# Two-layer SSD, attention and expert kernel: gather table, place of the gate exponent, and one set of transposes

## The reference

```python
def peer_ffn(h, w_q, keys, u_tab, v_tab):            # 8 heads, top 16, 128 x 128 experts
    q = (ht @ w_q).reshape(t, PEER_HEADS, 2, PEER_HALF)
    sc = jnp.einsum('thid,hikd->thik', q, keys)
    top_s, top_i = lax.top_k(sc, PEER_TOPK)
    cand = top_s[:, :, 0, :, None] + top_s[:, :, 1, None, :]
    best_s, best_pos = lax.top_k(cand.reshape(...), PEER_TOPK)
    experts = i1 * N_KEYS + i2
    gates = jax.nn.softmax(best_s, axis=-1)
    act = jnp.einsum('thkd,td->thk', u_tab[eb], hb)
    coef = gb * jax.nn.gelu(act, approximate=False)
    return jnp.einsum('thk,thkd->td', coef, v_tab[eb])
```

## Time and profile before

| | |
|---|---|
| median of three runs | 3040.66 us |
| the profiled execution | 3040.0 us |
| its span | 3038.2 us |
| TensorE matmuls busy | 2956.2 us, 97% of the span |
| VectorE busy | 2545.0 us, 84% |
| ScalarE busy | 1471.2 us, 48% |
| POOL busy | 953.9 us, 31% |
| granted TensorE clock, mean | 0.993 |
| chain that ended last | TensorE 87%, VectorE 5%, DMA 4%, ScalarE 2% |

### The profile page before, as it was taken

How to read it: one execution, slowest core, us unless ns; L and a number is a source line. 1 busy time by engine, 2 the same in 40 slices (tenths; PEclk the granted TensorE clock), 3 DMA queues, 4 the chain that set the end, 5 groups by cost and what they waited for, 6 DMA issues and landing times.

```text
span 3038.2 us, 48402 instructions
## 1 busy us (share of the span) xinstructions
PE 2956.2 (97%) x17448; PEld 2750.6 (91%) x17448; DVE 2545.0 (84%) x4940; ACT 1471.2 (48%) x2352; POOL 953.9 (31%) x709
## 2 busy tenths in 40 slices
PE   6999999999999999999989989999999999999998
PEld 3766789999999999999977668999999999999997
DVE  4666789999897789899886769999989868899888
ACT  4343234488884333333353532446888733333333
POOL 1000026545444333233300000565544433333331
PEclk9999999999999999999999999999999999999999
DMA  7424646799999999999931112568999899999996
GB/s 273 173 90 166 250 147 204 249 331 385 348 360 351 346 358 349 362 364 354 351 100 65 53 63 84 158 204 317 352 381 379 300 384 347 360 364 351 362 358 220
DMA packets 252361, 836.75 MB, mean 275 GB/s; under 512 B 24640, under 2 KB 57664, under 8 KB 241472
## 3 DMA queue, kind: packets, MB, share of 16 engines
q1 hardware_dynamic: 158336, 453.50, 42.0%
q0 software_dynamic: 89280, 348.17, 31.0%
q10 hardware_dynamic: 4608, 33.56, 2.6%
HBM read 751.24 MB, written 83.89 MB: 275 GB/s over the span
## 4 chain that ended last, share of the span: by engine, by line
PE 87%; DVE 5%; DMA 4%; ACT 2%; issue 1%; SPq 0%; POOL 0%; DVEq 0%; ACTq 0%
PE bank L962 41%; PE bank L1449 30%; PE bank L1417 5%; PE bank L1260 3%; DMA w_raw<-wst 3%; PE bank L978 2%; DVE w_lo L1491 1%; PE bank L1018 1%; ACT w_hi L680 1%; PE bank L1340 1%; PE bank L1236 1%; DMA pj<-adaw 1%; DMA ring<-u,gidx 1%; DVE vacc L1988 1%; PE bank L1431 0%
## 5 line engine op out<-in xcount | busy, mean ns | idle before, releaser
L680 ACT ACTIVATE w_hi<-w_raw 128x1024 fp32r<-128x1024 f32 x596 | 630.5, 1058 | 833.4 <-PE bank L962 640.5
L1491 DVE TENSOR_TENSOR w_lo<-w_raw,w_hi 128x1024 fp32r<-128x1024 f32 x522 | 638.8, 1224 | 345.3 <-ACT w_hi L680 335.0
L962 PE MATMUL bank<-hH,w_hi 128*128 128x368 f32 (+1 forms) x2528 | 881.6, 349 | 7.8 <-ACT w_hi L680 5.2
L962 PE MATMUL bank<-hH,w_lo 128*128 128x368 f32 (+1 forms) x2528 | 861.1, 341 | 0.0
L962 PE MATMUL bank<-hL,w_hi 128*128 128x368 f32 (+1 forms) x2528 | 860.7, 340 | 0.0
L1449 PE MATMUL bank<-c_hi,w_hi 128*128 128x368 f32 x2048 | 676.2, 330 | 4.3 <-DVE w_lo L1491 4.2
L1449 PE MATMUL bank<-c_lo,w_hi 128*128 128x368 f32 x2048 | 674.3, 329 | 0.0
L1449 PE MATMUL bank<-c_hi,w_lo 128*128 128x368 f32 x2048 | 673.1, 329 | 0.0
L644 POOL DMA_INDIRECT ring<-u,gidx x288 | 418.2, 1452 | 453.9 <-DVE gact L1976 421.1
L644 POOL DMA_INDIRECT ring<-v,gidx x288 | 331.9, 1152 | 694.3 <-DVE vacc L1988 632.7
L962 PEld LDWEIGHTS bank<-hH,w_hi 128*128 128x128 f32 x2528 | 475.4, 188 | 53.0 <-issue 21.2
(11 more groups left out here) (314 smaller groups left out, 2968.5 us busy)
## 6 DMA issues: line engine op xcount, KB each, us to landing
w_raw<-wst SPq DMA_DIRECT2D x596, 512.0 KB
activations<-act_out SPq DMA_DIRECT2D x128, 368.0 KB
act_in<-activations SPq DMA_DIRECT2D x64, 736.0 KB
gate_matrices<-stage ACTq DMA_DIRECT2D x32, 1024.0 KB
gates<-gate_matrices SPq DMA_DIRECT2D x64, 512.0 KB
ada_buf<-adaw POOLq DMA_DIRECT2D x24, 1024.0 KB, 7.0
nrm<-adaw POOLq DMA_DIRECT2D x8, 1024.0 KB, 5.2
pj<-adaw POOLq DMA_DIRECT2D x7, 1024.0 KB, 7.1
```

The costliest lines, as they stand in the source:

```text
L680: nc.scalar.activation(w_hi[g % 2][:, :, :].rearrange("p a b -> p (a b)"), w_raw[:, g % RAWS, :], ACT.Copy).then_inc(s_wh, 1)
L962: last = mm(bank[s][:, 0:t.stop - t.start], a[s][:, k, :], b[:, k, t], start=(k == 0 and a is w_hi and b is hH), stop=(k == KT - 1 and a i ...
L1491: v.tensor_tensor(w_lo[g % 2][:, :, :].rearrange("p a b -> p (a b)"), w_raw[:, g % RAWS, :], w_hi[g % 2][:, :, :].rearrange("p a b -> p (a ...
```

## The change

First, the table of gathers: tiles 37 to 43 take two each throughout, and the rule that gave two to every tile with n % 16 = 12 is dropped. With the filling up to 144 the counts are:

| tiles | before | now |
|---|---|---|
| 37 | 2 | 3 |
| 38, 39, 40 | 2, 2, 2 | 2, 2, 2 |
| 41, 42, 43 | 1, 1, 1 | 2, 2, 2 |
| 44, 60, 76, 92 | 2 each | 1 each |
| all others | | unchanged |

Second, ScalarE's exponent of a block's gates stands behind the Gelu of U tile 10·tt + 4 instead of 10·tt + 6 for tt = 1, 2 and 3, and stays at tile 6 for tt = 0. Third, the eight transposes that spread the extra tokens' activations are written as ordinary matmuls with the identity as the moving operand. The loops over both layers make each edit act twice.

```diff
 for _n in range(GATHER0, GATE0):
-    U_GATHERS[_n] = 2 if _n < GATHER0 + 4 else 1
+    U_GATHERS[_n] = 2
 for _n in range(GATE0, GATE1):
-    U_GATHERS[_n] = 2 if len(quads_of(_n + 1)) < 2 or _n % GATE_LOOP == 0 or _n % 16 == 12 else 1
+    U_GATHERS[_n] = 2 if len(quads_of(_n + 1)) < 2 or _n % GATE_LOOP == 0 else 1
...
-                    if tt < NT and m == 6:
+                    if tt < NT and m == (6 if tt == 0 else 4):
                         act.wait_ge(s_shift, l * NT + tt + 1)
                         nc.scalar.activation(bestv[:, :, :], bestv[:, :, :], ACT.Exp).then_inc(s_gexp, 1)
...
                     for k in range(KT):
-                        last = nc.tensor.transpose(bank[6 + k // 4][:, k % 4 * P:(k % 4 + 1) * P],
-                                                   htok2[:, k * P:(k + 1) * P], ident[:, :])
+                        last = mm(bank[6 + k // 4][:, k % 4 * P:(k % 4 + 1) * P],
+                                  htok2[:, k * P:(k + 1) * P], ident[:, :],
+                                  start=True, stop=True)
```

## The result

The changed kernel took 3058.64 us (median of 4 runs, 3054.8 to 3063.73) against 3041.13 for the kernel before on the same chip: a ratio of 1.0055, 95% interval 1.004 to 1.0072, about 17 us slower. The forecast, 3045.5 us with a range up to 3050, was too low by 13 us. The profiled execution took 3056.11 us, its span 3054.3 us against 3038.2.

A forecast was written before the change was run, and what follows sets the result against it. TensorE was taken to bound the kernel, busy 591.34 of 595 us in layer 0's expert tiles. Terms +2.5 +1.8 +1.6 -2.7 +3.0 -1.0 = +5.2 us on 3040.0 gave a forecast of 3045.5 us, range 3040 to 3050.

The forecast's parts named there:

- Edit 1's pauses: TensorE before tile 17: w_hi held behind the exponent's wait for scores, +2.5 us in layer 0, +1.8 in layer 1.
- B: VectorE's COPY ahead of block 1's scores stays long: +1.4 and +2.1 us more, 3049 us; chance 11%.
- C: ScalarE's stall does not reach TensorE, yet the waits at tile 39 go: 3038 us; chance 14%.
- Rival D: TensorE's clock falls to half rate in the new pause before tile 17: +1.7 to +3.4 us, 3048 us; chance 6%.
- 1.6 us predicted: TensorE's eight plain matmuls in place of transposes: +0.8 us per layer.
- the middle, 1.5 each: +3.0: Pause before quad 0 of tile 44, waiting for the fifteenth gather: 1.5 us per layer, bounds 0 and 4.
- Rival A: Gather supply gives out before quad 0 of tile 44; at 2.8 us spacing, +5 to +7 us more, 3051; chance 15%.
- The first gather starts at 575.5 in layer 0 and at 2057.1: VectorE's first gather starts earlier than before, from 577.04 to 575.5 in layer 0, 2059.77 to 2057.1 in layer 1.
- the anchor: Seventh gather comes 10.4 us (layer 1: 9.7) after the first slot's release, so at 587.1 and 2068.0.
- The discount: Pause before quad 0 of tile 44: 2.4 and 3.0 us cut to 1.5 each; sixth-gather count gave 0 to 1.8.
- Tile 39: TensorE's two waits before this tile, 1.35 us each with the slow restart, vanish: -2.7 us in all.
- Tile 80: Layer 0's 0.92 us wait there goes, VectorE being one gather ahead: -1.0 us.

The follow-up runs named there:

- Edit 1: Gate exponent moved from U tile 6 to 4 in blocks 1 to 3; alone against the kernel before: 3045.97 us, ratio 1.0017.
- Edit 2: Eight transposes written as plain matmuls; alone against the kernel before, run twice: 3046.01 us, ratio 1.0012, and 3045.63 us, ratio 1.0013.
- edit 3: New table of gathers per tile; alone against the kernel before: 3052.75 us, ratio 1.0032.

## Why the prediction was wrong

**Edit 1's pauses: right in size.** The steps can be read on ScalarE and VectorE of the changed kernel:

```profile
486.20 1.28 ACT L901 ACT_TABLE_LOAD   x1
491.39 0.31 ACT L901 ACTIVATE bestv<-bestv 128x128 f32<-128x128 f32 x1 [3.91 <-DVE bestv L2024]
491.61 1.04 ACT L680 ACTIVATE w_hi<-w_raw 128x1024 fp32r<-128x1024 f32 x1
```

```profile
490.86 0.17 DVE L2023 COPY gsum<-bestv 128x8 f32<-128x8 f32 x1
```

The COPY took 0.17 us, against 1.59 before, since POOL stood still behind the blocked w_hi, as the prediction took it. It was 0.17 us at this place in all twelve cases (six profiles, two layers) in which ScalarE held w_hi of tile 17. This bears out the Trainium skill, "SBUF — State Buffer", section "Who interferes with whom". The pauses of 2.70 and 2.05 us answer to 2.5 and 1.8. Rivals B and C fell with these rows.

**Rival D, the clock, was given 6% and is common.** In the six profiles with edit 1's early exponent in block 1 there are twelve pauses at tile 17, of 2.05 to 2.71 us, and the clock fell to 1.2 GHz for 3.4 us right behind nine of them. At tiles 39 and 41 and at the first quad, sixteen pauses of 2.00 to 2.85 us in all profiles had a fall in or behind five. The changed kernel's own profile has five such pauses and one fall, behind tile 17's in layer 1. Where it fell at tile 17, tile 20 was 1.6 us later than where it did not (4.3 against 2.7 us lost in layer 0, 3.5 or 3.6 against 2.0 in layer 1), near the 1.7 worked out. The evidence against D was that the clock held through pauses of 1.2 us; it held through all pauses of the U tiles under 2.0 us here, so those of 2 us and more are another case. Why it falls behind one and not the next stays open.

**Edit 2: right.** 1.6 us predicted for both layers, 1.8 measured. The Trainium skill's factor of four ("TensorE: Matmul & The Clock Gate", Terms) would have given +2.9 a layer; the runs show 1.87 against 0.97 us, a factor of 1.9.

**The step that failed: "the middle, 1.5 each: +3.0" for edit 3's supply, and under it the path to the first gather.** It measured 1.86 + 2.29 us in layer 0 and 2.00 + 2.14 in layer 1: 8.3 us, just above the bound of 4 per layer that I had set. The waits behind it are on VectorE (layer 0; the last rows are the thirteenth and the fifteenth gather):

```profile
583.20 1.23 DVE L1977 CUSTOM_DVE_ANT_0 ring<-ring,htok 128x1024 f32<-128x1024 f32 x1 [2.42 <-issue]
...
595.44 1.22 DVE L1977 CUSTOM_DVE_ANT_0 ring<-ring,htok 128x1024 f32<-128x1024 f32 x1 [2.89 <-DMA ring<-u,gidx]
598.07 1.23 DVE L1977 CUSTOM_DVE_ANT_0 ring<-ring,htok 128x1024 f32<-128x1024 f32 x1 [0.27 <-DMA ring<-u,gidx]
600.14 1.23 DVE L1977 CUSTOM_DVE_ANT_0 ring<-ring,htok 128x1024 f32<-128x1024 f32 x1 [0.84 <-DMA ring<-u,gidx]
...
608.27 1.23 DVE L1977 CUSTOM_DVE_ANT_0 ring<-ring,htok 128x1024 f32<-128x1024 f32 x1 [1.09 <-DMA ring<-u,gidx]
...
613.35 1.23 DVE L1977 CUSTOM_DVE_ANT_0 ring<-ring,htok 128x1024 f32<-128x1024 f32 x1 [1.55 <-DMA ring<-u,gidx]
```

and on POOL, whose w_lo of tile 38 stands ahead of them all:

```profile
580.67 2.39 POOL L632 TENSOR_TENSOR w_lo<-w_raw,w_hi 128x1024 fp32r<-128x1024 f32 x1 [1.67 <-ACT w_hi L680]
584.71 1.69 POOL L644 DMA_INDIRECT ring<-u,gidx  x1 [1.65 <-DVE gact L1977]
```

Its parts, one by one:
- The spacing was not too short. The seventh to fifteenth gather came 17.9 / 8 = 2.24 us apart in layer 0 (595.44 to 613.35), 2.22 in layer 1, against the 2.4 and 2.6 taken from the earlier trace rows. Rival A had the right pauses (4 to 5 a layer) for the wrong reason, a spacing of 2.8. The 10.4 and 9.7 us of the kernel before, with the 1.2 of a gather's use, over five buffers would have given 2.3 and 2.2, an estimate nearer than the spacings of the earlier trace rows.
- What stands behind the fifteenth was right: 3.78 us to the quad in both layers, 3.6 predicted.
- "The first gather starts at 575.5 in layer 0 and at 2057.1" failed, and with it the anchor. It started at 583.20, 2.4 us after the routing ended (580.61 + 0.17): VectorE waits at L2095 for POOL's w_lo of tile 38, and that goes by TensorE's pace. Before, it was done at 575.1 (2057.8 in layer 1), ahead of the routing, so no row showed a wait. With the 3.3 and 2.6 us by which the prediction itself delayed TensorE, it is done at 578.4 and 2060.4, 2.9 and 3.3 us after the gathers were to start. Edit 1 alone shows the same hold, 2.39 and 2.57 us. The prediction moved TensorE later and VectorE earlier, and did not ask what ties them. Its gather led tile 39 by 7.1 us (575.5 to 582.6); in the changed kernel the lead is 4.8 (583.20 to 587.97), and that with a pause in it.
- The seventh came 11.0 us after the first slot was freed (584.4 to 595.4), 11.3 in layer 1, not 10.4 and 9.7. The sixth landed 5.0 us after its issue, the seventh to fifteenth 8.0 to 9.9. What made the seventh's way longer than before is not shown.
- The discount failed too. The working from the seventh gather gave 2.4 and 3.0 us; I took 1.5 for both, because counting from the sixth gave less. Put together with the measured parts, layer 0 comes out: 2.4, + 3.1 for the lead over tile 39 (7.1 against 4.8, of which 0.7 is tile 39's pause), + 0.6 to the seventh, - 1.5 for the spacing, + 0.2 behind the fifteenth, - 0.7 since tile 39's pause is counted by itself: 4.1 us, measured 4.15. In layer 1 the same gives 3.0 + 3.5 + 1.6 - 3.0 + 0.2 - 0.7, less 0.4 since TensorE itself took longer to the quad: 4.2, measured 4.14. So the late first gather is the largest term in both layers.
- Tile 41 had no term. By my figures the seventh gather (587.1) left its w_lo ready a microsecond ahead of TensorE in layer 0; measured, the gather started at 595.44, w_lo at 596.59, and the tile at 597.91.

**Tile 39: -2.7 predicted, -1.3 measured.** With the old table the pauses vanish (edits 1 and 2 alone), so the outcome is right for edits 1 and 2, but by luck: the first gather is not at 575.5. With edit 1 alone it starts at 579.88, held, and w_lo of tile 39 ends at 583.4; the pause is gone only because TensorE, 4.6 us late by then, comes at 583.9. The third gather at tile 37, behind a first gather that is held, leaves 0.7 in each layer. **Tile 80:** -1.0 predicted, and the pause at 803.84 is gone; with edit 1 alone 0.3 us of it is left, so the table need not be the cause.

**The sum again:** 2.70 + 2.05 + 1.8 - 1.3 + 8.3 - 1.1 = 12.5 us, and 1.6 for the clock behind tile 17 of layer 1: 14.1, where the U tiles of the profile lost 13.3. Against the forecast's +5.2, 5.3 of the missing 8.9 us are the supply, 1.6 the clock, 1.4 tile 39 and 0.6 small ones. The medians say 16.7 (0.0055 of 3041), interval 12 to 22, which holds both. Whether the fall at 220 us, in the rest of the profile's 16.1, is more frequent in the changed kernel stays open: it is in its one profile and in neither of the two of before.

## What to carry to other kernels

When an edit moves work earlier on one engine, look for waits that cost nothing before on that engine and on the one that issues its transfers: a step cannot be earlier than the last of them, and removing one bares the next. A stage that already waits for its transfers has no room for more of them; count transfers per tile against their spacing before moving any. And a new pause of 2 to 3 us in dense TensorE work should be priced with a chance of a clock fall behind it; here it came in 14 of 28 cases.

## What the runs showed of the hardware

- TensorE's granted clock fell to 1.2 GHz for 3.4 us in or behind 14 of 28 pauses of 2.00 to 2.85 us in the U tiles (nine of twelve at tile 17, five of sixteen elsewhere), and behind none of the shorter ones. A fall at tile 17 cost 1.6 us.
- In sparse attention work the clock stood at half for 6.8 us at about 220 us in some executions of a kernel and not in others (edit 2's two profiles). Across it 2.7 to 2.9 us were lost against the kernel before.
- VectorE's 128x1024 multiply and sum took 1.22 us, and 3.40 to 3.42 us where it met POOL's subtraction, which takes 2.4 us by itself and took 3.35 in one of the two.
- The seventh to fifteenth gathers, 512 KB each, took 8.0 to 9.9 us from issue to landing with the DMA engines 98% busy (357 GB/s) and weight loads beside them; those of 256 KB took 3.8 to 7.8 us in the same place. The full ones reached VectorE 2.2 us apart, with a ring of five.
